# An mLSTM stage between a projection and attention: where masks, exponentials and key weights are computed, and when loads start

## The reference, cut to what matters

```
b = cumsum(lf);  a_inter = b + m
d = where(tril, b[t] - b[s] + li[s], NEG_INF)
m_t = max(a_inter, max(d));  w_inter = exp(a_inter - m_t)
s = exp(d - m_t) * (q_t . k_s)
num = w_inter * (C q_t) + s v;  den = w_inter * (n . q_t) + sum(s)
h = num / max(|den|, exp(-m_t))
C_new = decay * C + sum(exp(g - m_new) v k^T);  n likewise
```

## Time and profile before

| | us |
|---|---|
| median of 3 timed runs (3481.07 to 3484.96) | 3482.3 |
| time of the profiled execution | 3476.55 |
| its span | 3474.8 |
| PE busy in the span (94%) | 3264.0 |
| VectorE busy (60%) | 2085.5 |
| ScalarE busy (37%) | 1302.6 |
| GpSimd busy (12%) | 404.7 |

### The profile page before, as it was taken

One profiled execution on the slowest core, in us unless ns is written; L12 is line 12 of the kernel. 1 busy time (PEld: TensorE's weight loads), 2 busy tenths in 40 slices (PEclk: granted clock), 3 DMA queues, 4 the chain that ended last, 5 costly groups with the idle time before them and its releaser, 6 DMA issues.

```text
span 3474.8 us, 39492 instructions
## 1 busy us (share of the span) xinstructions
PE 3264.0 (94%) x16006; PEld 2680.3 (77%) x16006; DVE 2085.5 (60%) x2663; ACT 1302.6 (37%) x1876; POOL 404.7 (12%) x505
## 2 busy tenths in 40 slices
PE   6999999999998679999999999889989999998998
PEld 3788888878696568878888888767868887786887
DVE  7555555554753779665555555653258886225986
ACT  3222222232322158532222222552137754214772
POOL 0000000021011112120100001001001200100120
PEclk8999999999998789999999999999999999999999
DMA  4222222216345159312222222214433412443431
GB/s 196 85 97 73 85 85 85 85 62 118 125 170 177 37 96 103 79 49 73 97 97 85 73 87 95 63 66 133 115 75 65 59 37 90 130 115 79 63 57 61
DMA packets 137365, 315.18 MB, mean 91 GB/s; under 512 B 55152, under 2 KB 72304, under 8 KB 126176
## 3 DMA queue, kind: packets, MB, share of 16 engines
q1 hardware_dynamic: 74960, 213.60, 19.1%
q0 software_dynamic: 62224, 99.05, 13.6%
HBM read 261.52 MB, written 51.10 MB: 90 GB/s over the span
## 4 chain that ended last, share of the span: by engine, by line
PE 85%; DVE 7%; ACT 4%; issue 2%; DMA 2%; POOL 1%; SPq 0%; DVEq 0%; ACTq 0%; POOLq 0%
PE psum L833 36%; PE psum L950 12%; PE psum L919 11%; PE psum L1241 6%; PE psum L1255 5%; PE psum L1231 4%; PE psum L1355 4%; PE psum L961 3%; ACT attn_num L1822 1%; PE psum L1059 1%; PE psum L1065 1%; PE psum L1455 1%; ACT attn_th L1813 1%; DVE w_lo L2060 1%; DVE ada_acc L2077 1%
## 5 line engine op out<-in xcount | busy, mean ns | idle before, releaser
L2060 DVE TENSOR_TENSOR w_lo<-w_raw,w_hi 128x1024 fp32r<-128x1024 f32 (+1 forms) x131 | 218.6, 1669 | 338.2 <-ACT w_hi L1488 338.2
L833 PE MATMUL psum<-a_hi,w_hi 128*128 128x512 f32 x704 | 276.3, 392 | 6.0 <-DVE a_lo L2182 3.8
L833 PE MATMUL psum<-a_lo,w_hi 128*128 128x512 f32 x704 | 274.9, 390 | 0.0
L833 PE MATMUL psum<-a_hi,w_lo 128*128 128x512 f32 x704 | 274.9, 390 | 0.0
L1241 PEld LDWEIGHTS psum<-mats,attn_num 128*128 128x128 f32 x1536 | 169.7, 144 | 115.8 <-ACT attn_num L1822 90.2
L2569 DVE TENSOR_TENSOR attn_tl<-psum,attn_th 128x512 fp32r<-128x512 f32 x384 | 247.1, 684 | 17.1 <-ACT attn_th L1813 13.3
L1813 ACT ACTIVATE attn_th<-psum 128x512 fp32r<-128x512 f32 x384 | 209.4, 597 | 125.6 <-PE psum L1241 120.2
L1241 PE MATMUL psum<-mats,attn_num 128*128 128x128 f32 x1536 | 215.0, 284 | 39.6 <-ACT attn_num L1822 29.6
L2250 DVE SCALAR_TENSOR_TENSOR x<-psum,cols,x 128x1024 f32<-128x1024 f32 x144 | 184.4, 1282 | 94.4 <-PE psum L833 94.3
L1488 ACT ACTIVATE w_hi<-w_raw 128x1024 fp32r<-128x1024 f32 (+1 forms) x131 | 183.8, 1403 | 142.9 <-PE psum L833 39.6
L2563 DVE TENSOR_REDUCE attn_sm<-psum 128x1 f32<-128x1024 f32 x128 | 156.0, 1220 | 31.5 <-PE psum L1231 31.4
(11 more groups left out here) (567 smaller groups left out, 8414.5 us busy)
## 6 DMA issues: line engine op xcount, KB each, us to landing
w_raw<-in_w_ada SPq DMA_DIRECT2D x52, 1024.0 KB, 4.8
w_raw<-in_w_gu SPq DMA_DIRECT2D x44, 1024.0 KB, 4.8
w_raw<-in_w_in SPq DMA_DIRECT2D x34, 1024.0 KB, 5.1
w_raw<-in_w_down SPq DMA_DIRECT2D x22, 1024.0 KB, 4.9
w_raw<-in_w_out SPq DMA_DIRECT2D x12, 1024.0 KB, 8.2
qk_hi_scratch<-p_out_hi POOLq DMA_DIRECT2D x18, 512.0 KB, 3.0
qk_lo_scratch<-p_out_lo POOLq DMA_DIRECT2D x18, 512.0 KB, 3.8
w_early<-in_w_ada SPq DMA_DIRECT2D x8, 1024.0 KB, 18.2
```

The source lines that it names most:

```text
L833: mm = e.matmul(bank, a[:, k * width + m * P:k * width + (m + 1) * P], b(k, h), start=(ends[0] and k == order[0] and i == 0), stop=(ends[1 ...
L2060: e.tensor_tensor(like(src, lo), src, like(src, hi.bitcast(F32)), ALU.subtract).then_inc(*w_done.mark(n, part))
```

## The change

- *Loads and fences.* VectorE and ScalarE no longer stop at `fence("mlstm")` for each other and for the stores; they wait only for PE. The waits for the two stores move to the first place where a tile over the staging tiles is written: the squares of head 0 on ScalarE, the first division on VectorE. `first_heads` moves up on GpSimd, before the wait for head 2's output; it now waits for PE's last `kv` of head 3 and last `l` of head 2. `attention_tiles` without `between` puts its tiles in another order. VectorE's `ml_drained` stands at u = 4.
- *Masks.* `causal` now adds the table in place to the loaded maxima, as soon as these have landed. The sum with the key's column is gone from VectorE.
- *Exponentials.* ScalarE's `ml_decay` makes 8 activations of 128x128 for a direction, with the key's column as bias. For heads 2 and 3 it now waits for PE's `l` of head h-2, and SP's reload waits for these activations.
- *Weights of the keys.* `ml_weighted` moves from VectorE to ScalarE: 8 activations of 128x64 for a direction, with the column of `colsB` as scale. They stand before `ml_decay` of the same head, and for head 0 right behind the key copy.

```diff
@@ attention_tiles
-        a.q = rings(f"{name}_q", 2, [P, S], F32R, scope)
-        a.kh, a.kl, a.v = [], [], []
-        for i in range(2):
-            if i == 1 and between is not None:
...
+            for kind, i in (("q", 0), ("kh", 0), ("q", 1), ("kh", 1)):
+                one(kind, i)
+            late = [sb(f"{name}_{kind}1", shape, F32R, scope) for kind, shape in (("kl", [P, S]), ("v", [P, ST, P]))]
+            a.nu = rings(f"{name}_num", 2, [P, S], F32, scope)
+            gap(name, 2 * 1024, scope)
+            one("kl", 0)
+            one("v", 0)
@@ PE ml_prepare
-                    e.wait_ge(*ml_dve.at("kw", h, dr))
+                    e.wait_ge(*ml_act.at("kw", h, dr))
@@ ScalarE proj1
+                        ml_keys(0)
+                        ml_weighted(0)
                         for dr in range(2):
                             ml_decay(0, dr)
-                        ml_keys(0)
...
-            fence("mlstm")
-            for j in range(st.n - 2, st.n):
-                e.wait_ge(*st_stored[j % 2].at("p1b", j))
+            here("ACT", "mlstm")
+            e.wait_ge(*passed("PE", "mlstm"))
@@ ScalarE
         def ml_decay(h, dr):
-            E = t.ml.E[h % 2][dr]
+            m, row, E = t.ml, 32 * dr + h, t.ml.E[h % 2][dr]
             e.wait_ge(*ml_masked.at(h, dr))
-            e.activation(E[:], E[:], ACT.Exp).then_inc(*ml_act.mark("E", h, dr))
+            if h >= 2:
+                e.wait_ge(*ml_pe.at("l", h - 2, dr, 4))
+            for c in range(ST):
+                e.activation(E[:, c, :], (m.nb[dr] if h else E)[:, c, :], ACT.Exp,
+                             bias=m.colsA[:, c, row:row + 1]).then_inc(*ml_act.mark("E", h, dr))
+        def ml_weighted(h):
+            m = t.ml
+            for dr in range(2):
+                row = 32 * dr + h
+                e.wait_ge(*(ml_pe.at("kv", h - 1, 4, dr) if h else ml_act.now()))
+                for c in range(ST):
+                    e.activation(m.kw[dr][:, c, :], m.ktok[:, c, h * 64:(h + 1) * 64], ACT.Identity,
+                                 scale=m.colsB[:, c, 64 + row:64 + row + 1]).then_inc(*ml_act.mark("kw", h, dr))
         def ml_prepare(h):
             if h % 2 == 0:
                 if h:
                     ml_keys(h // 2)
+                    e.wait_ge(*ml_act.now())
                 yield
+            if h:
+                ml_weighted(h)
...
         def ml_norm(h):
+            if h == 0:
+                e.wait_ge(*st_stored[1].at("p1b", 11))
@@ VectorE (ml_decay and ml_weighted are gone with their calls)
-            fence("mlstm")
-            for j in range(11, 13):
-                e.wait_ge(*st_stored[j % 2].at("p1b", j))
+            here("DVE", "mlstm")
+            e.wait_ge(*passed("PE", "mlstm"))
...
+                        if h == 0 and c0 == 0:
+                            e.wait_ge(*st_stored[0].at("p1b", 12))
...
-                if u == 7 and masked:
+                if u == 4 and masked:
                     ml_drained(e)
@@ GpSimd
-                E, table = m.E[h % 2][dr], m.mats[:, (1 + dr) * P:(2 + dr) * P]
-                e.wait_ge(*ml_dve.at("E", h, dr))
+                E, table = (m.nb if h else m.E[0])[dr], m.mats[:, (1 + dr) * P:(2 + dr) * P]
+                e.wait_ge(*minus_M_in[2 + dr if h else dr].at(h))
                 e.tensor_tensor(E[:], E[:], table.unsqueeze(1).to_broadcast([P, ST, P]), ALU.add).then_inc(*ml_masked.mark(h, dr))
...
                 if h + 2 < M_HEADS:
                     causal(h + 2)
+                else:
+                    e.wait_ge(*ml_pe.at("kv", M_HEADS - 1, 4, 1))
+                    e.wait_ge(*ml_pe.at("l", M_HEADS - 2, 1, 4))
+                    first_heads("attn1", t.mix1.at)
                 e.wait_ge(*ml_dve.at("out", h))
...
-        e.wait_ge(*passed("PE", "ml early"))
-        first_heads("attn1", t.mix1.at)
@@ SP
-                    e.wait_ge(*ml_dve.at("E", h - 1, dr))
+                    e.wait_ge(*ml_act.at("E", h - 1, dr))
                     minus_M(m.nb[dr], h, dr, 2 + dr)
```

51 lines of the change are left out of this document (15 added, 36 removed).

## The result

| | us |
|---|---|
| before, median of 4 (3480.38 to 3484.96) | 3481.69 |
| changed kernel, median of 4 (3449.56 to 3460.41) | 3456.39 |
| ratio, 95% interval | 0.9922 [0.9906, 0.9937] |
| profiled execution after: time, span | 3453.12, 3451.3 |
| the same kernel once more, median of 5 (3456.10 to 3461.49), before 3478.14 | 3459.74 |

By these ratios the change takes off 27.2 us (21.9 to 32.7) and, once more, 20.9 us (16.3 to 25.4); the medians differ by 25.3 and 18.4. The forecast was 19.0 less.

The account below looks back on a forecast made before the run. The prediction took PE to bound the kernel, busy 94%, except in the 144 us mLSTM stage, where VectorE works nearly all the time. 7.8 - 2.0 + 3.3 + 2.5 + 7.4 = 19.0 us off 3482.3 gave 3463.3, range 3453 to 3475.

Parts of the forecast that it names:

- Piece 1: mLSTM stage's start up to head 0's first denominator: that denominator comes at 1119.5 instead of 1127.27, gain 7.8 us.
- The collision: GpSimd's masks of head 2 hold VectorE's divisions of head 0 at their shared SBUF port: loss 2.0 us.
- T: Time of the last absolute value of head 0, 1140.00 us in the kernel before.
- Piece 2: Turn from head 1 to head 2: first state at T+11.0 instead of T+13.3, PE wait of 0.98 gone; gain 3.3 us.
- Piece 3: Turn from head 2 to head 3: first state at T2+13.1 instead of T2+15.6; gain 2.5 us.
- T2: Time of the last absolute value of head 1, 1172.25 us in the kernel before.
- Piece 4: Attention's start: earlier q, k, v loads remove VectorE's idle time before its first maximum; gain 7.4 us.
- The tail: Stretch from head 3's first state to attention's first maximum; forecast 44.2 us, against 51.6 before.
- Short activations don't overlap: Rival: ScalarE's 88 short activations on the path cost 0.11 us more each, 9.7 lost, 3473; chance 0.14.
- They are cheaper, and no mask hits: Rival: short activations cost 0.08 us less each and no mask delays VectorE; 7.7 more gained, 3455.6; chance 0.14.
- PE's clock at attention: Rival: PE stays longer at 1.2 GHz in attention's first steps, costing 5 to 7.6 us, 3469; chance 0.10.
- It doesn't do what it says: Rival: absolute value behind 16 exponentials delays VectorE as the sums did, loads gain little; 3480; chance 0.04.

Follow-up runs that it names:

- Fence_only: Changed kernel with sums, masks, single exponentials, weighings and loads as before; only the waits at the stage's start, the tiles' order and u = 4 stay changed; 3466.10 us.
- old_masks: Changed kernel with key-column sums on VectorE, masks behind those sums and whole exponentials put back; 3459.84 us.
- Weights_dve: Changed kernel with only the key weighings put back on VectorE, two of 128x512 a head; 3457.40 us.
- loads_only: Kernel before the change, with only the change's early attention loads, tile order and u = 4; 3472.14 us.
- late_loads: Changed kernel with attention's first q, k, v loads put back behind all of PE's products of the stage; 3463.38 us.
- both_warm: Changed kernel with head 1's masks earlier, exponentials behind the first absolute value and squares, and head 3's first key product made five times; 3451.78 us.
- act_order: Changed kernel with ScalarE's exponentials of the next head moved behind the first absolute value and the turn's squares; 3457.83 us.

## Why the prediction was right, and where not

Forecast 3463.3, range 3453 to 3475, against 3456.39: faster, as said, and within the range, 7 lower. The stage's sum was 19.0 and it gave 19.8 and 18.7. But this is made of terms that missed in opposite ways.

*Piece 1, 7.8: it gave 11.2 (11.4 once more).* The order of the chain was as described: store, two loads, masks, exponentials, absolute value, division, with VectorE idle 5.5 before it. Off were the sizes. The copy wasn't 1.2 late, since sixteen weighings took 4.1 for 4.8, sixteen exponentials 4.8 for 5.6, and PE ended behind them. The first mask took 2.33 for 2.78: 0.5 (the second is over before its exponentials come, in the forecast as in the trace). Behind it the sixteen exponentials ran in one burst: 0.8, with their table loaded ahead: 1.3. With the copy's 1.2 these are 3.8; the masks began 0.5 later behind the projection's end (13.6 for 13.1 without the 1.2), which leaves 3.3 of the difference of 3.4. Fence_only shows what the waits alone give to this piece: 12.7, so the rest of the change took 1.5 back here; old_masks, 19.3 for 20.9, puts it down to masks and exponentials. I had priced the new chain against the old, and not each part against the others.

*The collision, 2.0: one hit of 1.6.* The nearest value, one hit, held. From the first denominator to T the changed kernel takes 15.0 for 12.7, 2.2 more.

The collision shows twice in VectorE's timeline, at 1119.28 and at 1160.30. The Trainium skill, SBUF — State Buffer, section "SBUF: two separate sides", has the shared port pair held for a whole instruction by whoever starts first; the trace agrees at 1119.28. At 1160.30 the VectorE sum started 0.4 us before the masks, and was held all the same, across two of them; neither the order of starts nor the unit of one instruction, as that section has them, gives 5.59 us. It cost VectorE nothing here: its next step behind the numerators waited until 1168.49 for ScalarE's squares, and these began at 1167.84, held by the exponentials ahead of them and not by this sum, which ended at 1165.89.

*Piece 2, 3.3: 3.6 (1.8 once more, at the lower clock). Piece 3, 2.5: 3.7 (3.7).* The sums came at T+8.4 for the forecast T+9.5: 24 activations, each 0.05 cheaper, are 1.2. They came at T2+10.4 for T2+11.6: the second mask of head 3 was done at T2+7.2 instead of 7.8 or later, and the exponentials behind it were cheaper. Weights_dve bears out what ScalarE's weighings give in piece 3, 2.7.

*Piece 4, 7.4: the idle time is gone whole,* as loads_only and late_loads show from both sides, and VectorE ends last there. *The step that failed is the sentence before it:* "After it, head 3's outputs: no step of the change touches them, VectorE has 44 us of its own work. I take 0." It had no check of its own: a stretch with the same instructions was taken to last as long. The tail took 48.0 instead of 44.2: 3.8 lost (3.7 once more), with PE at 1.2 GHz until 1208 and VectorE waiting for it, 3.21 at 1185.37. The clock was a rival only for attention, where it cost 1.3 (28.8 for 27.5), and I had placed it where PE would stop; it came 48 us earlier, in a stretch whose instructions the change leaves alone. PE had even been busier just ahead of it, 8.68 of 11.9 us, where the kernel before has 3.21 of 15.6. That the loss goes with the clock is shown by all fourteen profiles, which fall into tails of 44.1 to 45.2 and of 47.6 to 48.6. The change did touch something here, by the weighings: the lower clock came in seven of eight profiles with ScalarE's weighings and in none of four with VectorE's. Why isn't settled: late_loads had 0.84 in the same place with the same instructions, and both_warm had not, with the product repeated.

Together: 11.2 - 2.2 + 3.6 + 3.7 + 7.4 - 3.8 = 19.9, or 19.8 before rounding. That this lies so near to 19.0 is luck in part: piece 1 and piece 3 gave 4.6 more than priced, and the tail took 3.8 of it back.

*The rivals.* "Short activations don't overlap" (3473) fell: all did. "They are cheaper, and no mask hits", 3455.6, was the nearest in its time, and half right: 0.25 and 0.29 apart for my 0.30 and 0.35; one mask hit. ScalarE was never the bound of the stage, but in one sense it was what ended last twice, as act_order shows: by place in its queue, not by price. "PE's clock at attention" came in small, 1.3 for the 5 to 7.6 priced; "It doesn't do what it says" fell: the first denominator came 11.2 earlier in spite of the 5.5 us that VectorE waited for the exponentials. What the timed runs have beyond the stage, 27.2 for 19.8, stays unexplained; the repeat, 20.9 for 18.7, has 2.2.

The Trainium skill, ScalarE: Activation LUTs, section "What ACT_TABLE_LOAD costs", has 280 ns + 0.833 ns per element for an activation with one column, and an overlap of 93 ns between neighbours: as an estimate 0.387 and 0.333 alone, 0.29 and 0.24 apart. The trace agrees: 0.386 and 0.332 alone, 0.29 and 0.25 apart. I had drawn on the same page's rule for authors, which has no overlap; by this section, as an estimate, the copy isn't late (1.2) and sixteen exponentials cost 0.9 less, which puts piece 1 at 9.9 instead of 7.8.

## What to carry to other kernels

When an engine takes over work, look first at what small operation stands behind it in that engine's queue: here 16 exponentials ahead of a 0.2 us absolute value, and a mask behind a store that it didn't need, cost 6 to 8 us of a stage that the change had shortened by 20, and one moved line gave them back in the stage, though the timed runs can't confirm it. In a stage where TensorE waits often, a change that moves its waits can go with another clock: price each of its products at both levels before writing "0", and keep the difference (here 3.8 us) in the range. Undo each part alone as well as do it alone: of the stage, the early waits gave 11 us alone, VectorE's 3 as the last part, and the masks and exponentials nothing.

## What the runs showed of the hardware

- Short activations with one column start 0.25 us (128x64) and 0.29 us (128x128, SBUF) apart, 0.33 and 0.39 alone; a semaphore signal on each doesn't keep them from overlapping.
- A table load can run ahead of the wait of the activation that needs it (1100.23, the activation then waited 8.04 us for the mask); in fence_only's kernel it ran behind that wait (1110.87, after 13.58). Why wasn't looked into.
- A VectorE sum with both operands in SBUF that starts 0.4 us before two GpSimd masks took 5.59 us for 0.69; another behind a mask's start was held 1.6 us, until its end.
- With the same instructions, one execution had a granted clock of 0.50 from 1170 to 1190 us and another 0.84; in the first PE was busy 17.9 of the 20 us, in the other 12.8. Over fourteen profiles the tail took 44.1 to 45.2 us where its first 20 us had 0.84 or more, and 47.6 to 48.6 where they had 0.68 or less.
